# A state-space scan whose direct matrix is made in column tiles and placed by DMA, with half of its stage's weight splits moved to another engine

## What is computed

```
def s5_mixer(h, w_in, lam_re, lam_im, log_step, b_re, b_im, c_re, c_im, d_skip, w_glu, b_glu, w_out):
    u, z = jnp.split(h @ w_in, 2, axis=-1)
    lam_bar = jnp.exp(lam * step)
    b_bar = ((lam_bar - 1.0) / lam)[..., None] * lax.complex(b_re, b_im)
    ug = u.reshape(bsz, T, S5_GROUPS, S5_GROUP).astype(jnp.complex64)
    bu = jnp.einsum('gpi,btgi->btgp', b_bar, ug)
    a_seq = jnp.broadcast_to(lam_bar, (1, T, S5_GROUPS, S5_STATE))
    _, states = lax.associative_scan(_diag_linear_combine, (a_seq, bu), axis=1)
    y = jnp.einsum('gip,btgp->btgi', c, states).real.reshape(bsz, T, S5_WIDTH) + d_skip * u
    y = jax.nn.gelu(y)
    ...
```

## Time and profile before

| | |
|---|---|
| runs | 3425.39, 3428.21, 3429.63 us; median 3428.21 |
| profiled execution | 3431.38 us, its span 3429.7 |
| granted TensorE clock, mean | 0.993 |
| PE busy | 3337.7 us, 97% of the span |
| DVE busy | 2389.4 us, 70% |
| ACT busy | 1549.9 us, 45% |
| POOL busy | 233.5 us, 7% |
| the scan's chunks | from the first L2690 at 1672.40 us of the span to the last at about 1970 |

### The profile page before, as it was taken

One profiled execution on the slowest core, in us unless ns is written; L12 is line 12 of the kernel. 1 busy time (PEld: TensorE's weight loads), 2 busy tenths in 40 slices (PEclk: granted clock), 3 DMA queues, 4 the chain that ended last, 5 costly groups with the idle time before them and its releaser, 6 DMA issues.

```text
span 3429.7 us, 47776 instructions
## 1 busy us (share of the span) xinstructions
PE 3337.7 (97%) x18278; PEld 2905.2 (85%) x18278; DVE 2389.4 (70%) x3146; ACT 1549.9 (45%) x1911; POOL 233.5 (7%) x273
## 2 busy tenths in 40 slices
PE   8999999999999999999999999999998999999998
PEld 7888888878888878888999998899996888888887
DVE  6877777786555575766899967777657666556566
ACT  4444444444444344443687754444433443443442
POOL 0000000010000012730100000000001100000000
PEclk9999999999999999999999999999999999999999
DMA  6455555544544453443433356645444555555553
GB/s 243 172 185 184 184 183 182 201 171 182 184 172 176 180 186 135 175 164 144 145 119 116 117 199 222 203 159 178 169 159 163 186 188 191 185 190 188 184 190 128
DMA packets 91091, 598.43 MB, mean 174 GB/s; under 512 B 10785, under 2 KB 10865, under 8 KB 30001
## 3 DMA queue, kind: packets, MB, share of 16 engines
q1 hardware_dynamic: 83520, 557.88, 45.3%
q0 software_dynamic: 7408, 38.33, 3.2%
HBM read 590.84 MB, written 5.32 MB: 174 GB/s over the span
## 4 chain that ended last, share of the span: by engine, by line
PE 66%; issue 15%; DVE 13%; DVEq 4%; ACT 2%; POOL 0%; ACTq 0%; DMA 0%; POOLq 0%
PE banks L731 18%; PE banks L733 18%; PE banks L732 18%; DVE WL L698 3%; DVE xc L1424 1%; PE banks L749 1%; PE banks L750 1%; PE banks L751 1%; DVEq L2667 1%; PE banks L1594 1%; DVE stats L828 1%; PE banks L1069 1%; DVEq L2657 1%; DVE xc L1421 1%; PE banks L3322 1%
## 5 line engine op out<-in xcount | busy, mean ns | idle before, releaser
L698 DVE TENSOR_TENSOR WL<-raw,WH 128x2048 fp32r<-128x2048 f32 (+2 forms) x565 | 1191.2, 2114 | 463.2 <-ACT WH L690 449.4
L690 ACT ACTIVATE WH<-raw 128x2048 fp32r<-128x2048 f32 (+2 forms) x575 | 1017.1, 1774 | 768.1 <-PE banks L733 685.9
L731 PE MATMUL banks<-WH,XH 128*128 128x512 f32 (+2 forms) x2784 | 1056.9, 380 | 24.4 <-POOL WL L714 8.5
L733 PE MATMUL banks<-WH,XL 128*128 128x512 f32 (+2 forms) x2784 | 1033.5, 371 | 0.0
L732 PE MATMUL banks<-WL,XH 128*128 128x512 f32 (+2 forms) x2784 | 1031.9, 371 | 0.0
L731 PEld LDWEIGHTS banks<-WH,XH 128*128 128x128 f32 x2784 | 526.3, 189 | 109.5 <-issue 20.7
L733 PEld LDWEIGHTS banks<-WH,XL 128*128 128x128 f32 x2784 | 525.8, 189 | 81.0
L732 PEld LDWEIGHTS banks<-WL,XH 128*128 128x128 f32 x2784 | 526.5, 189 | 77.8 <-issue 1.9
L731 PE MATMUL banks<-WH,YH 128*128 128x512 f32 x976 | 387.6, 397 | 2.3 <-DVE YL L2769 2.0
L733 PE MATMUL banks<-WH,YL 128*128 128x512 f32 x976 | 380.4, 390 | 0.0
L732 PE MATMUL banks<-WL,YH 128*128 128x512 f32 x976 | 380.2, 390 | 0.0
(11 more groups left out here) (456 smaller groups left out, 3567.5 us busy)
## 6 DMA issues: line engine op xcount, KB each, us to landing
raw<-in_stream SPq DMA_DIRECT2D x447, 1024.0 KB, 4.8
raw<-in_stream SPq DMA_DIRECT2D x68, 768.0 KB, 4.1
raw<-in_stream SPq DMA_DIRECT2D x60, 512.0 KB, 3.5
gain<-in_gains POOLq DMA_DIRECT2D x9, 1024.0 KB, 5.1
arow<-acs_scratch POOLq DMA_DIRECT2D x8, 1024.0 KB, 5.0
offs<-in_ln_b POOLq DMA_DIRECT2D x4, 1024.0 KB, 7.7
acc<-in_x SPq DMA_DIRECT2D x2, 1024.0 KB, 7.2
turns_scratch<-trig POOLq DMA_DIRECT2D x16, 128.0 KB, 2.0
```

Source lines behind the costliest of these rows:

```text
L690: nc.scalar.activation(WH[:, n.first % PARTS, at], raw[:, n.first % RING, at], ACT.Copy).then_inc(hi_ready, 1)
L698: nc.vector.tensor_tensor(WL[:, n.first % RING, at], raw[:, n.first % RING, at], WH[:, n.first % PARTS, at].bitcast(F32), ALU.subtract).th ...
L731: nc.tensor.matmul(out, xh[:, k0 + k, at], wh[:, k, lo:hi], start=start, stop=False)
L733: ins = nc.tensor.matmul(out, xl[:, k0 + k, at], wh[:, k, lo:hi], start=False, stop=stop)
```

## The change

The direct matrix is written by PE in four column tiles, so that the four groups of a chunk land in four partition groups of bank 4 (128 partitions by 128) instead of side by side in partitions 0 to 31. DVE copies it, with the skip added, to SBUF (`dn5`) in the middle of the scan, in the new `direct(c)`; POOL stores dn5 to a DRAM scratch and loads it back in four DMAs into the blocks of dt5 (`place_direct`). ACT's copies and DVE's `skip` go. The split of slot 7+2c goes from DVE to POOL in two halves, around the four DMAs. `select` makes both parts of a table at once, from rows [b, a, -b] that ACT writes (`rows_of_chunk`). DVE waits for POOL's split ahead of its own.

```
         def direct_of(c):
             pe.wait_ge(csel_ready, c + 1)
-            for j in range(4):
-                for x in range(2):
-                    ins = nc.tensor.matmul(bank[4][0:32, j * P:j * P + P], bs5[:, x, j, 0, :],
+            pe.wait_ge(wb_ready, c + 1)
+            for x in range(2):
+                for j in range(4):
+                    ins = nc.tensor.matmul(bank[4][32 * j:32 * j + 32, 0:P], bs5[:, x, j, 0, :],
                                            cs5[:, x, j, 0:4, :].rearrange("p n i -> p (n i)"),
                                            start=x == 0, stop=x == 1)
...
         def outputs_of(c):
             pe.wait_ge(state_made, c + 1)
-            pe.wait_ge(direct_ready, c + 1)
+            pe.wait_ge(direct_ready, 16 * 4 * (c + 1))
...
-        def direct(c):
-            act.wait_ge(direct_done, c + 1)
-            view = bank[4][0:32, :].rearrange("p (j w) -> p j w", j=4)
-            for q in range(4):
-                at = slice(32 * q, 32 * q + 32)
-                ins = nc.scalar.activation(dt5[at, :, 32 * (3 - q):P], view[:, :, 0:32 * (q + 1)], ACT.Copy)
-            ins.then_inc(direct_copied, 1)
+        def rows_of_chunk(c):
+            four = slice(4 * c, 4 * c + 4)
+            if c:
+                act.wait_ge(csel_ready, c)
+            for kind, (source, one, two) in enumerate(((c5, 1, 0), (b5, 0, 1))):
+                nc.scalar.activation(rows5[:, kind, :, 0, :], source[:, one, four, :], ACT.Copy)
+                nc.scalar.activation(rows5[:, kind, :, 1, :], source[:, two, four, :], ACT.Copy)
+                ins = nc.scalar.activation(rows5[:, kind, :, 2, :], source[:, one, four, :], ACT.Copy, scale=-1.0)
+            ins.then_inc(rows_ready, 1)
...
-            if c:
-                direct(c)
             split_high(act, At(n + 7 + 2 * c))
             if c + 1 < CHUNKS5:
+                rows_of_chunk(c + 1)
                 trig(c + 1)
...
+            nc.vector.tensor_tensor(t1, lo, re if kind else im, ALU.mult)
+            nc.vector.tensor_tensor(t2, hi, im if kind else re, ALU.mult)
+            dve.drain()
+            for h in range(2):
+                at = slice(64 * h, 64 * h + 64)
+                out = target[at, :, :, 0:powers, 16 * h:16 * h + 16].rearrange("p x j n i -> p (j n) x i")
+                nc.vector.tensor_tensor(out, t1[at].rearrange("p j n (x i) -> p (j n) x i", x=2),
+                                        t2[at].rearrange("p j n (x i) -> p (j n) x i", x=2), ALU.add)
...
             nc.vector.tensor_tensor(w5[:, 2:4, :], v, sin, ALU.mult).then_inc(v_read, 1)
-            dve.drain()
+            direct(c)
...
-        def skip(c):
-            dve.wait_ge(direct_copied, c + 1)
-            for j in range(4):
-                ins = nc.vector.scalar_tensor_tensor(dt5[:, j, :], jump5[:, :], d5[:, 4 * c + j:4 * c + j + 1], dt5[:, j, :],
-                                                     ALU.mult, ALU.add)
-            ins.then_inc(direct_ready, 1)
+        def direct(c):
+            dve.wait_ge(direct_done, c + 1)
+            if c:
+                dve.wait_ge(direct_stored, 16 * c)
+            nc.vector.scalar_tensor_tensor(dn5[:, 0:32], jump5[:, :], d5[:, c:c + 1], bank[4][:, 0:32], ALU.mult, ALU.add)
+            nc.vector.tensor_copy(dn5[:, 32:P], bank[4][:, 32:P])
+            dve.drain().then_inc(direct_copied, 1)
...
             scan(c)
-            skip(c)
-            split_low(dve, At(n + 7 + 2 * c))
             if c + 1 < CHUNKS5:
                 input_tables(c + 1)
+            dve.wait_ge(lo_ready, n + 8 + 2 * c)
             split_low(dve, At(n + 8 + 2 * c))
...
+        def place_direct(c):
+            pool.wait_ge(direct_copied, c + 1)
+            pool.dma_start(direct_dram[c], dn5[:, :]).then_inc(direct_stored, 16)
+            if c + 2 < CHUNKS5:
+                pool.wait_ge(trig_ready, c + 1)
+                pool.dma_start(turns5[:, c % 2, :], turns_dram[c + 2]).then_inc(turns_loaded[c % 2], 16)
+            low_half_of(pool, S5_SLOT + 7 + 2 * c, 0)
+            pool.wait_ge(direct_stored, 16 * (c + 1))
+            for q in range(4):
+                pool.dma_start(dt5[32 * q:32 * q + 32, :, 32 * (3 - q):P],
+                               direct_dram[c].rearrange("(j i) w -> i j w", j=4)[:, :, 0:32 * (q + 1)]).then_inc(direct_ready, 16)
+            low_half_of(pool, S5_SLOT + 7 + 2 * c, 1).then_inc(lo_ready, 1)
```

More of the change, by code:

```diff
@@ L44 @@
 MEM_HEADS = 4
+CHUNKS5 = 16
 FOX_SLOT = SSD_GROUPS * 16 + 1
@@ L270, in arrays @@
                           for k in ("s5_c_re", "s5_c_im")], 1).reshape(P, D),
-        "s5_d": np.ascontiguousarray(np.tile(one["s5_d"].reshape(64, 32).T, (4, 1))),
+        "s5_d": cols(one["s5_d"]),
         "s5_bglu": cols(one["s5_b_glu"]),
@@ L364, in program @@
         turns5 = sb("turns5", [P, 2, T], within=s)
-        jump5 = sb("jump5", [P, P], within=s)
+        jump5 = sb("jump5", [P, 32], within=s)
+        dn5 = sb("dn5", [P, P], within=s)
     sb("apart", [P, 24])
@@ L487, in program @@
         co5 = sb("co5", [P, 2, 64], within=s)
-        d5 = sb("d5", [P, 64], within=s)
+        d5 = sb("d5", [P, CHUNKS5], within=s)
         spare = small[:, :, :].rearrange("p c n -> p (c n)")
@@ L496, in program @@
         q4 = small[:, :, :].rearrange("p c n -> p (c n)").rearrange("p (a t) -> p a t", a=4)
+        rows5 = con[:, C_TRI:C_MASK].rearrange("p (k j r i) -> p k j r i", k=2, j=4, r=3)
     with ExitStack() as s:
@@ L614, in program @@
     direct_ready = sem("direct_ready")
+    direct_stored = sem("direct_stored")
+    rows_ready = sem("rows_ready")
     turns_stored = sem("turns_stored")
@@ L705, in first_lows, with low_half_of @@
             low_in_halves(pool, n)
+    def low_half_of(pool, n, h):
+        if h == 0:
+            pool.wait_ge(hi_ready, n + 1)
+            pool.wait_ge(lo_ready, n)
+        at = slice(h * SLOT // 2, (h + 1) * SLOT // 2)
+        return nc.gpsimd.tensor_tensor(WL[:, n % RING, at], raw[:, n % RING, at],
+                                       WH[:, n % PARTS, at].bitcast(F32), ALU.subtract)
     def low_in_halves(pool, n):
@@ L2351, in program @@
     TURN4, R4 = 0, 1
-    CHUNKS5 = 16
     BLOCK5 = [((i // 4) % 2, i % 4) for i in range(35)] + [(1, 0), (1, 1), (1, 2), (0, 3), (1, 3)]
@@ L2535, in keep_z @@
                                  ACT.Copy).then_inc(free[pair], 1)
+        act.wait_ge(s5_loaded, 64)
+        rows_of_chunk(0)
         split_high(act, At(n + 4))
@@ L2547, in s5_scalar @@
         stack(0, (1, 2), range(16))
-        direct(0)
         for c in range(CHUNKS5):
@@ L2642, in s5_vector, with select @@
         flat = q4.rearrange("p a t -> p (a t)")
-        def select(target, source, kind, powers, c):
+        def select(target, kind, powers, t1, t2, c):
             four = slice(4 * c, 4 * c + 4)
-            shape = [P, 4, powers, 16]
+            shape = [P, 4, powers, 32]
             re, im = (pows5[:, x, 0:powers, kind, four].rearrange("p n j -> p j n").unsqueeze(3).to_broadcast(shape)
                       for x in range(2))
[L2650 to L2656, removed]
-                dve.drain()
[L2658 to L2668, removed]
@@ new lines, in select @@
+            lo, hi = (rows5[:, kind, :, r:r + 2, :].rearrange("p j r i -> p j (r i)").unsqueeze(2).to_broadcast(shape)
+                      for r in range(2))
+            size = 4 * powers * 32
+            t1, t2 = (t[:, 0:size].rearrange("p (j n i) -> p j n i", j=4, i=32) for t in (t1, t2))
+            nc.vector.tensor_tensor(t1, lo, re if kind else im, ALU.mult)
[6 more added lines that the diff above has]
+                                        t2[at].rearrange("p j n (x i) -> p (j n) x i", x=2), ALU.add)
@@ L2670, in input_tables @@
         def input_tables(c):
+            dve.wait_ge(rows_ready, c + 1)
             if c:
                 dve.wait_ge(direct_done, c)
-            select(bs5, b5, 1, 4, c)
+            select(bs5, 1, 4, flat, flat[:, 512:1024], c)
             dve.drain().then_inc(bs_ready, 1)
@@ L2680, in output_tables @@
                 dve.wait_ge(y5_done, c)
-            select(cs5, c5, 0, 5, c)
+            select(cs5, 0, 5, flat, w5[:, :, :].rearrange("p a t -> p (a t)"), c)
             dve.drain().then_inc(csel_ready, 1)
@@ L2732, in s5_vector @@
             at = slice(32 * q, 32 * q + 32)
-            nc.vector.tensor_copy(jump5[at, 32 * (3 - q):32 * (3 - q) + 32], ident[at, 32 * q:32 * q + 32])
+            nc.vector.tensor_copy(jump5[at, :], ident[at, 32 * q:32 * q + 32])
         dve.drain()
@@ L2902, in s5_pool @@
         nc.gpsimd.memset(ring5[:, :, :].rearrange("p j k -> p (j k)"), 0.0)
-        nc.gpsimd.memset(jump5[:, :], 0.0)
         pool.drain().then_inc(zeroed, 1)
-        for c in range(2, CHUNKS5):
-            pool.wait_ge(trig_ready, c - 1)
-            pool.dma_start(turns5[:, c % 2, :], turns_dram[c]).then_inc(turns_loaded[c % 2], 16)
+        def place_direct(c):
[10 more added lines that the diff above has]
```

(3 more changed lines are left out.)

1 line of the change is left out of this document (added).

## The result

The changed kernel takes 3520.99 us (median of 4 runs, 3518.97 to 3521.67) against 3427.84 for the kernel before (4 runs): a ratio of 1.0265, 95% interval 1.0253 to 1.0277, **93 us slower**. The forecast had the sign, and a fifth of the size: +18, with a range that ended at 3468.

A forecast was written before the change was run, and what follows sets the result against it. VectorE was taken as the bound, 19.13 us a chunk. Stacking chunks +10, other ordinary chunks -3, last chunks +3.5 and clock +7 gave +17.5, so +18 on 3428.21: 3446 us, own range 3436 to 3457, wider range 3424 to 3468.

The forecast's parts named there:

- VectorE's own work: In each chunk of the scan, VectorE's work without waiting for POOL falls from 19.13 to 14.7 us.
- I take 2 x 2.0 = 4.0 a chunk: VectorE's instructions with two SBUF operands stand still for POOL's two halves, 4.0 us a chunk, bounds 0 and 4.8.
- rival (a): In the chunks POOL, not VectorE, does the waiting; TensorE becomes the bound, -12 us, 3417, faster; 15%.
- in its middle. So the scan ends at ... 8.2: POOL issues half 1 about 2.9 us into the scan, which then ends 8.2 us after its start.
- rival (b): Half 2 too falls in the scan, which ends at 10.2; 8 x 2 = +16 us in stacking chunks, 3462; 22%.
- The chain behind it: From the scan's end, ACT's sines, ring and stacking, the unstacking and the turned inputs take 10.25 us.
- In ordinary chunks the placement lands about 8.2 + 2 ... and I cost it at nothing: In ordinary chunks the placement DMAs land before or with TensorE's first products, costing nothing; landings 3 us later cost +2 a chunk.
- Rival (c): The placement lands late in every chunk, or most pauses cost clock: 13 x 2 or 20 us more, 3470 and up; 8%.
- It waits in one piece, ahead of inputs_of: In stacking chunks TensorE has 1.5 to 3.0 us to wait, in one pause ahead of inputs_of.
- the forecast's ring of scan, ACT and inputs_of: In stacking chunks 0 to 7 VectorE, ACT and TensorE together set a period of 20.4 us, +1.3 each, +10.
- +7 was taken for the clock: Half of TensorE's eight pauses bring 3.4 us at half clock, 1.7 lost each: +7 us, bounds 0 and 14.
- The last chunks, +3.5: Late placement costs +2.3 us at outputs_of in chunk 13 and +1.3 in chunk 14: +3.5.

The follow-up runs named there:

- x1: The change with POOL's two halves taken out and the split of slot 7+2c back on VectorE behind the scan: 3428.69 us, ratio 1.0002 to the kernel before.
- halves-alone kernel: The kernel before with only the split of slot 7+2c moved to POOL in two halves: 3461.69 us, ratio 1.0095.
- drained kernel: The change with a drain of POOL ahead of each half of the split: 3523.66 us, ratio 1.0276 to the kernel before.
- z2: The change with the store and the four placement DMAs issued by SyncE ahead of the weight load: 3480.88 us, ratio 1.0151 to the kernel before.
- filler: The change with 26 extra transposes in TensorE's pause ahead of outputs_of: 3506.68 us, ratio 1.0226 to the kernel before.

## Why the prediction was wrong

**VectorE's own work: right.** The tables, the skip, the new direct: 14.7 us a chunk was forecast with the split of slot 7+2c away. In x1's chunk from 1746.11 the period of 18.43, less 1.76 of waits and 2.2 for that split, is 14.5. The scan grew by 0.36 (6.09 against 5.73) where 0.4 was taken.

**"I take 2 x 2.0 = 4.0 a chunk": the mechanism right, the size too small.** VectorE did stand still for POOL's halves, and in the change POOL never for VectorE: 32 halves had a mean of 2397 ns, as long as elsewhere. So rival (a) is out. (Not everywhere: in the halves-alone kernel one half took 3.02.) But the row of 2.01 that the price came from had a VectorE instruction that arrived during a half, with 2.21 of it left by its row. In the change the holds are 2.80 (4.07 - 1.27) and 3.14 (3.83 - 0.69) in the chunk above, together 5.9, and 6.8 in those whose scan ends at 12.9. An instruction that comes up while POOL is still issuing the DMAs ahead of a half stands already: L2712 started at 1779.79, 0.87 before the half, and would have been through in 0.69. The Trainium skill, SBUF — State Buffer, section Who interferes with whom, has the loser blocked for the winner's whole instruction. The halves alone agree (4.2 for 4.8 of POOL's work); the 5.9 here is more than the two halves.

**Half 1 "in its middle. So the scan ends at ... 8.2": the step that failed first.** Half 1 began where it was forecast, 3.1 us into the scan. But half 2 fell in the scan as well, in every chunk but 13. That was rival (b), at 22%, priced at one more hold of 2.0 in stacking chunks only; the scan ended at 12.0 to 12.9, not 10.2. The chain behind it was right: 10.25 was forecast from the scan's end to the end of the turned inputs, and the chunks 4 and 6 show 10.07. But a scan that late sets the period of the chunks without stacking too, which the forecast had at 18.7 and which took 24.4 to 26.3.

**"In ordinary chunks the placement lands about 8.2 + 2 ... and I cost it at nothing": the other step that failed.** The last piece landed 12.2 to 13.1 us after the scan's start, not near 10.2. Half 1 stands ahead of the placement on POOL's queue and moves it across the issue of the next weight load: the two whose issue ends at 1780.1 and 1780.65, behind the load's at 1779.68, land 5 us later. Rival (c) named the late placement and gave it 8%, at +2 a chunk. Its landings of 3 us more were right; its price per chunk was not, for a late outputs_of is a pause of TensorE, with a fall of the clock behind it, and the unstacking, the turned inputs and the next scan all come after it. The drained kernel, whose scan ends at 8.1 or 6.1, shows it at +95.

**"It waits in one piece, ahead of inputs_of": the place was wrong.** The pauses are ahead of outputs_of, 2.9 to 3.9 us in every chunk from 1 to 12 where 2 were expected, and after each the clock was at half for 6.8 or 10.2 us, not for 3.4 in every second one. With the placement early and only the scan late (z2), TensorE does wait ahead of inputs_of, 19.4 us in 9 waits, so the forecast's ring of scan, ACT and inputs_of exists. The filler gave back 14 us, where +7 was taken for the clock.

**The last chunks, +3.5: too small.** In chunk 13 outputs_of started 12.84 after the scan's start, 2.3 later than before, as taken. But the pause ahead of it, 3.5, had half clock behind it, and the chunk took 5.6 more; chunk 14 took 5.35 more where 1.3 was taken.

**The way the chances were built.** (b) and (c) were separate cases of 22 and 8%. They had one common cause, a half 1 on POOL's queue that puts all behind it later than the scan and the loads allow, and came together. Each was priced as a delay added to the forecast; no case had two late inputs of one wait.

## What to carry to other kernels

A split on POOL wasn't free work beside VectorE: here 2.2 us of VectorE became 4.2 to 6.8 us in which VectorE stood still, and it paid in none of these kernels. Before moving work to an idle engine, list what is queued behind it there and what each of those things must come ahead of; here the small DMAs that TensorE waits for landed in time once they stood on the queue of the large ones, ahead of them in program order. When two inputs of one wait are late, undoing one may show nothing, as the drained kernel did: test each with the other early.

## What the runs showed of the hardware that was not expected

- VectorE's instructions with two SBUF operands stood still up to 1.7 us before POOL's half began by its own row, while POOL issued DMAs ahead of it; with no half behind them, the same issues held up nothing (x1, L2712 at 692 ns). With a drain between, an instruction ran undisturbed until the half began. The second scan of the pair, which came up 1.65 to 1.67 before half 2, was caught in chunks 1 to 3, 5, 9 and 12, with a scan end of 12.8 to 12.9, and got through in 4, 6, 7 and 10, with one of 12.0. Why the hold begins early wasn't shown; the profile's spans on POOL are rough.
- 64 KB or less, issued by POOL behind the issue of a 1 MB weight load, landed 3.6 to 5.1 us later, and ahead of it 1.9 to 2.4 (medians). In the drained kernel the late ones land about when the load does: in its chunks 1 to 13 the first piece lands 11.7 to 12.1 us after the scan's start, whether it is issued 7.5 or 9.2 after it; the load, issued at 6.7, takes a median of 5.0.
- Sixteen matmuls in four column tiles took 10.3/16 = 0.64 us a chunk (x1), against 2.0 one after the other, 3.1 times less.
